# Gate and up products of a two-layer trunk: activation columns streamed from the last to the first, weight buffers placed at four residues of 512 bytes

## The chip, the cores and the metric

The kernel runs on one core of a Trainium2 chip. The metric is the device time of one execution in microseconds (us). Engines are named as in the profile: PE is TensorE's matmul, PEld its weight load, DVE is VectorE, ACT is ScalarE, POOL is GpSimd, SP is the engine that issues most DMAs. A difference of about 2% (20.8 us here) is taken as what tells a change of this kernel from none.

## The reference

Two layers over 256 tokens of width 1024, each layer a SwiGLU block, a mixing block (windowed attention and low-rank attention, gated and merged), and a second SwiGLU block:

```python
def swiglu(x, w_gate, w_up, w_down):
    return (jax.nn.silu(x @ w_gate) * (x @ w_up)) @ w_down

for l in range(DEPTH):                      # DEPTH = 2, D_MODEL = 1024, SEQ = 256, D_FF = 2816
    x = x + 0.5 * swiglu(rms_norm(x, ffn1_norm[l]), ffn1_w_gate[l], ffn1_w_up[l], ffn1_w_down[l])
    h = rms_norm(x, mix_norm[l])
    proj = h @ w_in[l]
    ...
    x = x + merged @ w_out[l]
    x = x + 0.5 * swiglu(rms_norm(x, ffn2_norm[l]), ffn2_w_gate[l], ffn2_w_up[l], ffn2_w_down[l])
```

All values are float32. The gate and up products (`x @ w_gate`, `x @ w_up`), four times in the program, are what the change touches.

## The kernel before

Precision is kept by splitting each float32 operand into a high part, rounded to the type float32r that PE takes in one pass, and a low part, the rest. A product is then three: high by high, low by high and high by low.

A SwiGLU block of D_FF = 2816 is worked in FB = 22 blocks of 128 inner columns. For each block the queue of SP loads 2048 columns of gate and up weights (8 tiles of 128 x 128 for gate, then 8 for up) into `w_raw`, ACT copies them to `w_hi` (function `split_gu`, line 549), and DVE writes the difference to `w_lo` (line 884). Both have two such buffers, slot 0 for even blocks and slot 1 for odd ones, and a third that holds the split weights of the down projection. The transposed activations `hT` hold, for each of the 8 chunks k of 128 model columns, 256 high columns and behind them 256 low ones.

On PE the gate and up products take the weights as the stationary operand and the activations as the moving one, with two helpers. `high` multiplies a `w_hi` tile by all 512 columns of `hT[k]` (in the profile: ps<-hT,w_hi, 128x512) and `low` a `w_lo` tile by the 256 high ones (ps<-hT,w_lo, 128x256). A block has 16 of each. Every product loads its own weights, and all of them are written at line 1369. In the steady loop PE does `gate_up` (16 high, 16 low), `gate_up_low_first` (16 low, 16 high), and two `down` of 12 products each, in which the weights move (ps<-w_hi,aTh and the like, 128x512). The mixing block in between has projections that also move the weights, 512, 416 or 384 columns at a time, over stationary pieces of `hT` or of the attention output `oTh`.

The order of work on every engine is written out by hand, with semaphores between engines; the two slots are what lets ACT, DVE and SP work ahead of PE.

Where the tiles lie in a partition matters here. Tiles are allocated one behind another. In bytes modulo 512, `w_raw`, `w_hi`, `hT`, `aTh` and `aTl` all begin at the same residue, since the sizes ahead of them are multiples of 512. In what follows "offset" is the residue of a tile's address against that common one. A 128 x 128 weight tile takes 512 bytes in a partition, so the tiles of one buffer have one offset. `w_hi` has offset 0, and the gate and up tiles of `w_lo` have 480, by

```python
LO_SHIFT = 120
LO_SLOT = GU_COLS + 128
wl_gu = [w_lo[:, i * LO_SLOT + LO_SHIFT:i * LO_SLOT + LO_SHIFT + GU_COLS] for i in range(2)]
```

while the attention output (`oTh`, its high part, and `oTl`, its low part) and `ident` lie at offset 256.

Of the kernel before, what the change touches and what calls it, by code (L numbers as in the profile page):

```python
# [7 lines left out]
F32 = mybir.dt.float32  # L8
# [89 lines left out]
def build(nc, x_first_in, x_second_in, pos_in, cols_in, rows_in, w_ffn, w_proj, w_gate, w_uq, w_ukv, w_branch, w_out,  # L98
          masks_in, freq_in, out):
    with ExitStack() as ctx:  # L100
# [3 lines left out]
        def signal(name, per_layer, first=0):  # L104
# [8 lines left out]
        raw_gu, wh_gu = ([w[:, i * GU_COLS:(i + 1) * GU_COLS] for i in range(2)] for w in (w_raw, w_hi))  # L113
        wl_gu = [w_lo[:, i * LO_SLOT + LO_SHIFT:i * LO_SLOT + LO_SHIFT + GU_COLS] for i in range(2)]
        raw_d, wh_d = ([w[:, 2 * GU_COLS + i * DN_COLS:2 * GU_COLS + (i + 1) * DN_COLS] for i in range(2)]
                       for w in (w_raw, w_hi))
        wl_d = [w_lo[:, 2 * LO_SLOT + i * DN_COLS:2 * LO_SLOT + (i + 1) * DN_COLS] for i in range(2)]
        mix_raw, mix_hi = ([w[:, i * GU_COLS:(i + 1) * GU_COLS] for i in range(MIX_SLOTS)] for w in (w_raw, w_hi))
        mix_lo = [w_lo[:, i * LO_SLOT:i * LO_SLOT + GU_COLS] for i in range(MIX_SLOTS)]
        hT = sb("hT", [P, KC, 2, SEQ], F32R)  # L120
# [399 lines left out]
        def _(act):  # L520
# [4 lines left out]
            for l in range(DEPTH):  # L525
# [25 lines left out]
                def start_high(i):  # L551

                    act.wait_ge(start_in[i].sem, 16)
                    act.activation(wh_gu[0][:, start_cols(i)], raw_gu[0][:, start_cols(i)], ACT.Copy)\  # L554
                       .then_inc(start_hi.sem if i < 3 else hi_gu.sem, 1)

                def third_high(half):

                    part = slice(half * KC * P, (half + 1) * KC * P)
                    act.wait_ge(third_in.sem, 16)  # L560
                    act.wait_ge(gu_used.sem, gu_used.at(0, 0))
                    act.activation(wh_gu[0][:, part], third_raw[:, part], ACT.Copy)\
                       .then_inc((third_hi, hi_gu)[half].sem, 1)
# [141 lines left out]
                if l == 0:  # L705
# [7 lines left out]
                    for s, (landed, sig) in enumerate(((start_in[4], start_hi), (raw_gu_in[1], hi_gu))):  # L713
                        part = slice(s * KC * P, (s + 1) * KC * P)
                        act.wait_ge(landed.sem, 16)
                        act.activation(wh_gu[1][:, part], raw_gu[1][:, part], ACT.Copy).then_inc(sig.sem, 1)
                    act.wait_ge(ss_clear.sem, 1)
# [151 lines left out]
        def _(dve):  # L869
# [3 lines left out]
            for l in range(DEPTH):  # L873
# [7 lines left out]
                def split_gu(n, i2, e):  # L881
                    b = e % 2
                    dve.wait_ge(hi_gu.sem, i2 + hi_gu.at(n // 2, (0, FFN2_0)[n % 2] + e))
                    dve.tensor_tensor(wl_gu[b], raw_gu[b], wh_gu[b].bitcast(F32), ALU.subtract).then_inc(lo_gu.sem, 1)  # L884

                def split_second(n):

                    for half, sig in enumerate((lo_first, lo_gu)):
                        if n == 0 and half == 0:
                            dve.wait_ge(start_hi.sem, 4)  # L890
                        else:
                            dve.wait_ge(hi_gu.sem, hi_gu.at(n // 2, (0, FFN2_0)[n % 2] + 1))
                        part = slice(half * KC * P, (half + 1) * KC * P)
                        dve.tensor_tensor(wl_gu[1][:, part], raw_gu[1][:, part], wh_gu[1][:, part].bitcast(F32), ALU.subtract)\
                           .then_inc(sig.sem, 1)
# [5 lines left out]
                def third_low(half):  # L901

                    if half == 0:
                        dve.wait_ge(third_hi.sem, 1)
                    else:
                        dve.wait_ge(hi_gu.sem, hi_gu.at(0, 2))
                    part = slice(half * KC * P, (half + 1) * KC * P)
                    ins = dve.tensor_tensor(wl_gu[0][:, part], third_raw[:, part], wh_gu[0][:, part].bitcast(F32), ALU.subtract)
                    ins.then_inc((third_lo, lo_gu)[half].sem, 1)

                def start_low(i):
# [3 lines left out]
                    else:  # L915
                        dve.wait_ge(hi_gu.sem, hi_gu.at(0, 0))
                    dve.tensor_tensor(wl_gu[0][:, start_cols(i)], raw_gu[0][:, start_cols(i)],
                                      wh_gu[0][:, start_cols(i)].bitcast(F32), ALU.subtract)\
                       .then_inc(start_lo.sem if i < 3 else lo_gu.sem, 1)
# [447 lines left out]
        def _(pe):  # L1367
# [17 lines left out]
            for l in range(DEPTH):  # L1385
# [36 lines left out]
                def high(bank, hi, k, first, last=False):  # L1422

                    return mm(ps[:, bank, :], hi, hT[:, k, :, :].rearrange("p s n -> p (s n)"), first, last)

                def low(bank, lo, k, last, first=False):

                    return mm(ps[:, bank, 0:SEQ], lo, hTh[:, k, :], first, last)

                def gate_up(w, i2, e):  # L1430
# [3 lines left out]
                    for s in range(2):  # L1434
                        for k in range(KC):
                            c = (s * KC + k) * P
                            high(2 * b + s, wh_gu[b][:, c:c + P], k, k == 0)
                    pe.wait_ge(lo_gu.sem, i2 + lo_gu.at(l, (0, FFN2_0)[w] + e))
                    for s, sig in enumerate((gate_ps, gu_used)):
                        for k in range(KC):  # L1440
                            c = (s * KC + k) * P
                            ins = low(2 * b + s, wl_gu[b][:, c:c + P], k, k == KC - 1)
                        ins.then_inc(sig.sem, 1)

                def gate_up_low_first(w, i2, e):
# [4 lines left out]
                    for s in range(2):  # L1450
                        for k in range(KC):
                            c = (s * KC + k) * P
                            low(2 * b + s, wl_gu[b][:, c:c + P], k, False, k == 0)
                    for s, sig in enumerate((gate_ps, gu_used)):
                        for k in range(KC):
                            c = (s * KC + k) * P
                            ins = high(2 * b + s, wh_gu[b][:, c:c + P], k, False, k == KC - 1)
                        ins.then_inc(sig.sem, 1)

                def gate_up_last(w, e):  # L1460
# [3 lines left out]
                    for s, sig in enumerate((gate_ps, gu_used)):  # L1464
                        for k in range(KC):
                            c = (s * KC + k) * P
                            high(2 * b + s, wh_gu[b][:, c:c + P], k, k == 0)
                        for k in range(KC):
                            c = (s * KC + k) * P
                            ins = low(2 * b + s, wl_gu[b][:, c:c + P], k, k == KC - 1)  # L1470
                        ins.then_inc(sig.sem, 1)

                def gate_up_first(w):
# [4 lines left out]
                    for k in range(KC):  # L1478
                        if k == 2:
                            columns(l, 2 * w, 1)  # L1480
                        if k == 0:
                            pe.wait_ge(ht_hi.sem, ht_hi.at(l, 2 * w * KC))
                            for s in range(2):
                                c = s * KC * P
                                low(s, wl_gu[0][:, c:c + P], 0, False, True)
                        pe.wait_ge(ht_lo.sem, ht_lo.at(l, 2 * w * KC + k))
                        for s in range(2):
                            c = (s * KC + k) * P
                            high(s, wh_gu[0][:, c:c + P], k, False)
                        if k == 0:  # L1490
                            continue
                        for s, sig in enumerate((gate_ps, gu_used)):
                            c = (s * KC + k) * P
                            ins = low(s, wl_gu[0][:, c:c + P], k, k == KC - 1)
                            if k == KC - 1:
# [3 lines left out]
                def start_high_four(s, half):  # L1499
# [5 lines left out]
                    for k in range(4 * half, 4 * half + 4):  # L1505
                        if s == 0:
                            pe.wait_ge(ht_lo.sem, ht_lo.at(0, k))
                        c = (s * KC + k) * P
                        high(s, wh_gu[0][:, c:c + P], k, k == 0)

                def start_low_four(s, half):
# [5 lines left out]
                    for k in range(4 * half, 4 * half + 4):  # L1517
                        c = (s * KC + k) * P
                        ins = low(s, wl_gu[0][:, c:c + P], k, k == KC - 1)
                    if half == 1:  # L1520
# [20 lines left out]
                def gate_up_second(w):  # L1541

                    for s, sig in enumerate((gate_ps, gu_used)):
# [6 lines left out]
                        for k in range(KC):  # L1550
                            c = (s * KC + k) * P
                            high(2 + s, wh_gu[1][:, c:c + P], k, k == 0)
                            if l + w == 0 and s == 1 and k == 4:
# [3 lines left out]
                        for k in range(KC):  # L1557
                            c = (s * KC + k) * P
                            ins = low(2 + s, wl_gu[1][:, c:c + P], k, k == KC - 1)
                        ins.then_inc(sig.sem, 1)  # L1560
                def gate_up_third():

                    pe.wait_ge(up_sum.sem, up_sum.at(0, 0))
                    for s, sig, hi, lo in ((0, gate_ps, (third_hi.sem, 1), (third_lo.sem, 1)),
                                           (1, gu_used, (hi_gu.sem, hi_gu.at(0, 2)), (lo_gu.sem, lo_gu.at(0, 2)))):
                        pe.wait_ge(*hi)
                        for k in range(KC):
                            c = (s * KC + k) * P
                            high(s, wh_gu[0][:, c:c + P], k, k == 0)
                        pe.wait_ge(*lo)  # L1570
                        for k in range(KC):
                            c = (s * KC + k) * P
                            ins = low(s, wl_gu[0][:, c:c + P], k, k == KC - 1)
                        ins.then_inc(sig.sem, 1)
# [410 lines left out]
```

## Time and profile before

| | us |
|---|---|
| median of 2 runs | 1039.09 (1038.88 to 1039.29) |
| the profiled execution's own time | 1040.34 |
| its span, first to last instruction | 1038.5 |
| PE busy | 1032.4 (99%), 5648 products |
| PE weight loads busy | 891.7 (86%) |
| DVE busy | 718.3 (69%) |
| ACT busy | 586.1 (56%) |

The busy time of PE covers the span, but a product's duration in the profile overlaps that of the next one: what a product costs is the step from its start to the start of the next, and this is what is read below. Times are given to 10 ns in the rows by time, so steps are taken over several products.

### The profile page before, as it was taken

What the parts mean: (1) busy time and instruction counts of PE and PEld (TensorE: products, weight loads), DVE (VectorE), ACT (ScalarE), POOL (GpSimd) and SP (SyncE); (2) the same over time, 40 slices, a digit from 0 to 9 for tenths busy, and PEclk for the clock granted to TensorE, in tenths of its full rate; (3) what the DMA queues carried; (4) which work ended last, traced back from release to release, by engine and by line L of the source; (5) the groups of instructions that cost most, each with busy time, mean ns of one, the idle gap of its engine ahead of it and who ended that gap; (6) DMA issues with size and microseconds to landing.
All of it is one profiled execution on the core that took longest, in us unless ns stands there. A gap on an engine that the chain in (4) does not pass through costs nothing.

```text
span 1038.5 us, 15559 instructions
## 1 busy us (share of the span) xinstructions
PE 1032.4 (99%) x5648; PEld 891.7 (86%) x5648; DVE 718.3 (69%) x1132; ACT 586.1 (56%) x935; POOL 61.8 (6%) x71
## 2 busy tenths in 40 slices
PE   8999999999999999999999999999999999999998
PEld 7888888998888888888888888889988888888887
DVE  6766666668786876666687666666688868666665
ACT  6555454466963754554565455455678646454552
POOL 0052000121100000000000000001211000000000
PEclk9999999999999999999999999999999999999999
DMA  7665544455435455655445555534454346545541
GB/s 264 248 225 192 204 162 167 140 183 193 146 123 203 173 187 189 205 189 209 179 147 202 202 192 182 210 136 152 154 203 163 122 163 219 205 163 202 191 173 61
DMA packets 35269, 187.53 MB, mean 181 GB/s; under 512 B 4368, under 2 KB 4384, under 8 KB 20128
## 3 DMA queue, kind: packets, MB, share of 16 engines
q1 hardware_dynamic: 34992, 186.51, 51.0%
q0 software_dynamic: 240, 0.53, 0.2%
q8 instruction: 23, 0.38, 0.1%
q14 instruction: 14, 0.11, 0.0%
HBM read 185.98 MB, written 1.05 MB: 180 GB/s over the span
## 4 chain that ended last, share of the span: by engine, by line
PE 99%; DMA 1%; SPq 0%; DVE 0%; ACT 0%; issue 0%
PE ps L1369 96%; PE ps L1803 1%; PE ps L1393 1%; DMA w_raw<-in_w_ffn 1%; PE ps L1832 1%; PE ps L1868 0%; PE ps L1712 0%; PE ps L1704 0%; PE ps L1414 0%; DVE x_cols L999 0%; ACT w_hi L554 0%; SPq L318 0%; SPq L317 0%
## 5 line engine op out<-in xcount | busy, mean ns | idle before, releaser
L1369 PE MATMUL ps<-hT,w_hi 128*128 128x512 f32 x1408 | 341.3, 391 | 1.9 <-ACT w_hi L554 1.9
L1369 PEld LDWEIGHTS ps<-hT,w_hi 128*128 128x128 f32 x1408 | 258.9, 188 | 52.4 <-ACT w_hi L554 2.1
L884 DVE TENSOR_TENSOR w_lo<-w_raw,w_hi 128x2048 fp32r<-128x2048 f32 x82 | 188.0, 2293 | 87.7 <-ACT w_hi L549 87.7
L1369 PEld LDWEIGHTS ps<-hT,w_lo 128*128 128x128 f32 x1408 | 176.8, 188 | 7.5
L1369 PE MATMUL ps<-hT,w_lo 128*128 128x256 f32 x1408 | 178.3, 279 | 0.0
L1369 PE MATMUL ps<-w_hi,hT 128*128 128x512 f32 (+2 forms) x576 | 174.3, 377 | 0.0
L549 ACT ACTIVATE w_hi<-w_raw 128x2048 fp32r<-128x2048 f32 x85 | 162.0, 1906 | 13.9 <-PE ps L1369 13.2
L1369 PE MATMUL ps<-w_lo,aTh 128*128 128x512 f32 x352 | 137.2, 390 | 0.0
L1369 PE MATMUL ps<-w_hi,aTl 128*128 128x512 f32 x352 | 137.0, 389 | 0.0
L1369 PE MATMUL ps<-w_hi,aTh 128*128 128x512 f32 x352 | 136.8, 390 | 0.0
L578 ACT ACTIVATE S<-ps 128x256 f32<-128x256 f32 x88 | 33.7, 383 | 154.6 <-PE ps L1369 154.6
L1369 PEld LDWEIGHTS ps<-w_hi,hT 128*128 128x128 f32 x576 | 107.2, 188 | 15.9 <-DVE w_lo L878 1.3
L878 DVE TENSOR_TENSOR w_lo<-w_raw,w_hi 128x2048 fp32r<-128x2048 f32 (+3 forms) x50 | 94.9, 1905 | 33.6 <-ACT w_hi L537 33.3
L537 ACT ACTIVATE w_hi<-w_raw 128x2048 fp32r<-128x2048 f32 (+3 forms) x54 | 86.0, 1592 | 52.0 <-PE ps L1369 49.8
L572 ACT ACTIVATE w_hi<-w_raw 128x1024 fp32r<-128x1024 f32 x88 | 92.9, 1055 | 38.4 <-PE ps L1369 38.4
L1369 PE MATMUL ps<-w_lo,hT 128*128 128x512 f32 (+2 forms) x288 | 107.5, 373 | 0.0
L940 DVE TENSOR_TENSOR w_lo<-w_raw,w_hi 128x1024 fp32r<-128x1024 f32 x88 | 104.4, 1219 | 1.4 <-ACT w_hi L572 1.4
L946 DVE TENSOR_TENSOR S<-ps,S 128x256 f32<-128x256 f32 x88 | 37.1, 421 | 84.9 <-ACT S L578 84.8
L1369 PEld LDWEIGHTS ps<-w_hi,aTl 128*128 128x128 f32 x352 | 66.1, 188 | 13.9
L1369 PEld LDWEIGHTS ps<-w_hi,aTh 128*128 128x128 f32 x352 | 66.1, 188 | 13.5
L1369 PEld LDWEIGHTS ps<-w_lo,aTh 128*128 128x128 f32 x352 | 66.1, 188 | 13.0
L584 ACT ACTIVATE work<-work 128x256 f32<-128x256 f32 x88 | 36.7, 417 | 68.5 <-DVE work L953 68.5
(168 smaller groups left out, 952.9 us busy)
## 6 DMA issues: line engine op xcount, KB each, us to landing
w_raw<-in_w_ffn SPq DMA_DIRECT2D x85, 1024.0 KB, 4.9
w_raw<-in_w_ffn SPq DMA_DIRECT2D x90, 512.0 KB, 5.7
w_raw<-in_w_gate SPq DMA_DIRECT2D x16, 1024.0 KB, 5.1
w_raw<-in_w_proj SPq DMA_DIRECT2D x16, 592.0 KB, 4.4
w_raw<-in_w_branch SPq DMA_DIRECT2D x8, 1024.0 KB, 4.8
w_raw<-in_w_out SPq DMA_DIRECT2D x8, 1024.0 KB, 4.8
w_raw<-in_w_uq SPq DMA_DIRECT2D x4, 384.0 KB, 3.0
w_raw<-in_w_ffn SPq DMA_DIRECT2D x4, 256.0 KB, 6.6
```

The costliest lines, as they stand in the source:

```text
L537: act.activation(mix_hi[m][:, 0:ncols], mix_raw[m][:, 0:ncols], ACT.Copy).then_inc(hi_gu.sem, 1)
L549: act.activation(wh_gu[b], raw_gu[b], ACT.Copy).then_inc(hi_gu.sem, 1)
L572: act.activation(wh_d[b], raw_d[b], ACT.Copy).then_inc(hi_d.sem, 1)
L578: act.activation(folded[:, b, 0, :], ps[:, 2 * b, SEQ:2 * SEQ], ACT.Copy).then_inc(g_low.sem, 1)
L584: act.activation(silu[:, b, :], silu[:, b, :], ACT.Silu).then_inc(silu_done.sem, 1)
L878: dve.tensor_tensor(mix_lo[m][:, 0:ncols], mix_raw[m][:, 0:ncols], mix_hi[m][:, 0:ncols].bitcast(F32), ALU.subtract).then_inc(lo_gu.sem, 1)
L884: dve.tensor_tensor(wl_gu[b], raw_gu[b], wh_gu[b].bitcast(F32), ALU.subtract).then_inc(lo_gu.sem, 1)
L940: dve.tensor_tensor(wl_d[b], raw_d[b], wh_d[b].bitcast(F32), ALU.subtract).then_inc(lo_d.sem, 1)
L946: dve.tensor_tensor(folded[:, b, 0, :], ps[:, 2 * b, 0:SEQ], folded[:, b, 0, :], ALU.add)\
L1369: return pe.matmul(dst, w, m, start=start, stop=stop, skip_group_check=True)
L1393: ins = pe.transpose(dst[:, t * P:(t + 1) * P], x[:, c // 4, t, c % 4 * P:(c % 4 + 1) * P], ident[:, :])
L1803: ins = pe.transpose(ps[:, 4 + h % 4, s * P:(s + 1) * P], S[:, h, s * P:(s + 1) * P], ident[:, :])
```

## The change

Three things change in the code, and all of them concern only the gate and up products.

- `high` and `low` read the activations from the last column to the first, and write their outputs in PSUM in the same reversed order, so each result stands where it stood before.
- `w_hi` gets the padded slots that `w_lo` had (2176 columns, 17 times 512 bytes, in place of 2048), and in both buffers the eight gate tiles and the eight up tiles of a slot begin at places of their own: offset 0 for gate and 256 for up in slot 0, offset 128 for gate and 384 for up in slot 1. The offset of 480 in `w_lo` is gone.
- Since gate and up no longer follow each other without a gap, the ACT copy and the DVE difference over 2048 columns write (and read) `w_hi` and `w_lo` in two pieces of 1024. The tiles behind `w_hi` move by 1536 bytes, three times 512, so no other offset changes.

```diff
-LO_SHIFT = 120
-LO_SLOT = GU_COLS + 128
+HI_AT, LO_AT = ((0, 64), (32, 96)), ((0, 64), (32, 96))
+PART_SLOT = GU_COLS + 128
...
-        w_hi = sb("w_hi", [P, MIX_SLOTS * GU_COLS], F32R)
-        w_lo = sb("w_lo", [P, MIX_SLOTS * LO_SLOT], F32R)
...
+        w_hi = sb("w_hi", [P, MIX_SLOTS * PART_SLOT], F32R)
+        w_lo = sb("w_lo", [P, MIX_SLOTS * PART_SLOT], F32R)
+        raw_gu = [w_raw[:, i * GU_COLS:(i + 1) * GU_COLS] for i in range(2)]
+
+        def halves(w, i, gate_at, up_at):
+
+            step = KC * P + up_at - gate_at
+            a = i * PART_SLOT + gate_at
+            return w[:, a:a + 2 * step].rearrange("p (s n) -> p s n", s=2)[:, :, 0:KC * P]
+
+        def cols_of(w, c, n):
+
+            return w[:, c // (KC * P), c % (KC * P):c % (KC * P) + n]
+
+        wh_gu, wl_gu = ([halves(w, i, *at) for i, at in enumerate(places)] for w, places in ((w_hi, HI_AT), (w_lo, LO_AT)))
...
-                    act.activation(wh_gu[b], raw_gu[b], ACT.Copy).then_inc(hi_gu.sem, 1)
+                    act.activation(wh_gu[b], raw_gu[b].rearrange("p (s n) -> p s n", s=2), ACT.Copy).then_inc(hi_gu.sem, 1)
...
-                    dve.tensor_tensor(wl_gu[b], raw_gu[b], wh_gu[b].bitcast(F32), ALU.subtract).then_inc(lo_gu.sem, 1)
+                    dve.tensor_tensor(wl_gu[b], raw_gu[b].rearrange("p (s n) -> p s n", s=2), wh_gu[b].bitcast(F32), ALU.subtract).then_inc(lo_gu.sem, 1)
...
-                    return mm(ps[:, bank, :], hi, hT[:, k, :, :].rearrange("p s n -> p (s n)"), first, last)
+                    return mm(ps[:, bank, :][:, ::-1], hi, hT[:, k, :, :].rearrange("p s n -> p (s n)")[:, ::-1], first, last)
...
-                    return mm(ps[:, bank, 0:SEQ], lo, hTh[:, k, :], first, last)
+                    return mm(ps[:, bank, 0:SEQ][:, ::-1], lo, hTh[:, k, :][:, ::-1], first, last)
```

All other edits put `cols_of` where a slice of `wh_gu` or `wl_gu` stood. No instruction is added, removed or moved on any engine: the lists of PE, POOL and SP are the same, and those of ACT and DVE differ only in the shape of the splits of 2048 columns. In ACT's list, in the loop of a SwiGLU block (`aTh` is the high part of the down projection's activations, S and work are scratch tiles), there stands before

```order
46 L549 ACTIVATE w_hi<-w_raw 128x2048
47 L597 ACTIVATE aTh<-work 128x256
48 L577 REGISTER_ALU
49 L578 ACTIVATE S<-ps 128x256
50 L589 REGISTER_ALU
51 L590 ACTIVATE S<-ps 128x256
```

and now

```order
46 L560 ACTIVATE w_hi<-w_raw 128x2x1024
47 L608 ACTIVATE aTh<-work 128x256
48 L588 REGISTER_ALU
49 L589 ACTIVATE S<-ps 128x256
50 L600 REGISTER_ALU
51 L601 ACTIVATE S<-ps 128x256
```

The instruction keeps its place and its neighbours, and only its form and the line numbers differ.

## Rows read from the trace of the kernel before

**Rows 1.** The page's head: busy time of each engine, and the granted clock by slices.

```profile
span 1038.5 us, 15559 instructions
PE 1032.4 (99%) x5648; PEld 891.7 (86%) x5648; DVE 718.3 (69%) x1132; ACT 586.1 (56%) x935; POOL 61.8 (6%) x71
...
PEclk9999999999999999999999999999999999999999
```

**Rows 2.** The page's chain of work that ended last, by engine and line.

```profile
PE 99%; DMA 1%; SPq 0%; DVE 0%; ACT 0%; issue 0%
PE ps L1369 96%; PE ps L1803 1%; PE ps L1393 1%; DMA w_raw<-in_w_ffn 1%; PE ps L1832 1%; PE ps L1868 0%; PE ps L1712 0%; PE ps L1704 0%; PE ps L1414 0%; DVE x_cols L999 0%; ACT w_hi L554 0%; SPq L318 0%; SPq L317 0%
```

**Rows 3.** All waits of PE: waiter, releaser, us in total, times, longest.

```profile
PE ps L1369 <- ACT w_hi L554: 1.9, 1, 1.9
PE ps L1380 <- DVE kTA L870: 1.0, 1, 1.0
```

**Rows 4.** The page's groups of the gate and up products and of their splits.

```profile
L1369 PE MATMUL ps<-hT,w_hi 128*128 128x512 f32 x1408 | 341.3, 391 | 1.9 <-ACT w_hi L554 1.9
...
L884 DVE TENSOR_TENSOR w_lo<-w_raw,w_hi 128x2048 fp32r<-128x2048 f32 x82 | 188.0, 2293 | 87.7 <-ACT w_hi L549 87.7
...
L1369 PE MATMUL ps<-hT,w_lo 128*128 128x256 f32 x1408 | 178.3, 279 | 0.0
...
L549 ACT ACTIVATE w_hi<-w_raw 128x2048 fp32r<-128x2048 f32 x85 | 162.0, 1906 | 13.9 <-PE ps L1369 13.2
```

**Rows 5.** PE by time, one turn of the loop: start us, us, products.

```profile
154.71 3.80 PE L1369 MATMUL ps<-hT,w_hi 128*128 128x512 f32 x16
158.34 3.90 PE L1369 MATMUL ps<-hT,w_lo 128*128 128x256 f32 x32
162.08 3.81 PE L1369 MATMUL ps<-hT,w_hi 128*128 128x512 f32 x16
165.73 0.39 PE L1369 MATMUL ps<-w_hi,aTh 128*128 128x512 f32 x1
...
171.17 3.80 PE L1369 MATMUL ps<-hT,w_hi 128*128 128x512 f32 x16
```

**Rows 6.** PE by time: mixing block, 384 columns a product.

```profile
202.41 0.51 PE L1369 MATMUL ps<-w_hi,hT 128*128 128x384 f32 x2
...
205.53 0.51 PE L1369 MATMUL ps<-w_hi,hT 128*128 128x384 f32 x2
```

**Rows 7.** PE by time: weights over `oTh` and `oTl`, which lie at offset 256.

```profile
303.14 0.39 PE L1369 MATMUL ps<-w_hi,oTl 128*128 128x512 f32 x1
...
305.86 0.39 PE L1369 MATMUL ps<-w_hi,oTl 128*128 128x512 f32 x1
```

**Rows 8.** Transposes of 128 columns on PE: two runs of twelve by time.

```profile
275.03 1.48 PE L1803 MATMUL ps<-ident,S 128*128 128x128 f32 x12
...
296.36 1.47 PE L1803 MATMUL ps<-ident,S 128*128 128x128 f32 x12
```

**Rows 9.** PE by line and form: all those transposes, busy us, mean ns.

```profile
L1803 PE MATMUL ps<-ident,S 128*128 128x128 f32 x96 | 11.8, 272 | 0.0
```

**Rows 10.** Writers of `oTh` (one piece of 512) and `hT` (two of 256): ns min/median/max.

```profile
L810 ACT ACTIVATE oTh<-ps x8: 574/594/598, 283.2 to 814.6; 128x512 fp32r<-128x512 f32 x8
L1275 DVE TENSOR_TENSOR oTl<-ps,oTh x8: 684/688/692, 285.7 to 815.3; 128x512 fp32r<-128x512 f32 x8
...
L853 ACT ACTIVATE hT<-ps x8: 594/596/598, 312.2 to 835.7; 128x512 fp32r<-128x512 f32 x8
L1305 DVE TENSOR_TENSOR hT<-ps,hT x8: 680/686/692, 312.8 to 836.5; 128x512 fp32r<-128x512 f32 x8
```

**Rows 11.** Busy time by stretch, that loop turn: PE, PEld, DVE, ACT, POOL, clock, DMA.

```profile
154.71:171.17 16.46, 16.46 (x90) 14.25 (x88) 10.75 (x15) 8.49 (x12) 0.00 (x0) 1.00 0.56 193
```

**Rows 12.** ACT and DVE by time: the split of the block that PE begins at 171.17.

```profile
161.40 1.91 ACT L549 ACTIVATE w_hi<-w_raw 128x2048 fp32r<-128x2048 f32 x1
...
163.34 2.29 DVE L884 TENSOR_TENSOR w_lo<-w_raw,w_hi 128x2048 fp32r<-128x2048 f32 x1 [0.85 <-ACT w_hi L549]
```

More of the change, by code:

```diff
@@ L110, in build @@
         w_raw = sb("w_raw", [P, MIX_SLOTS * GU_COLS])
-        w_hi = sb("w_hi", [P, MIX_SLOTS * GU_COLS], F32R)
-        w_lo = sb("w_lo", [P, MIX_SLOTS * LO_SLOT], F32R)
[L113 to L119, printed above, removed]
+        w_hi = sb("w_hi", [P, MIX_SLOTS * PART_SLOT], F32R)
[8 more added lines that the diff above has]
+        wh_gu, wl_gu = ([halves(w, i, *at) for i, at in enumerate(places)] for w, places in ((w_hi, HI_AT), (w_lo, LO_AT)))
+        raw_d = [w_raw[:, 2 * GU_COLS + i * DN_COLS:2 * GU_COLS + (i + 1) * DN_COLS] for i in range(2)]
+        wh_d, wl_d = ([w[:, 2 * PART_SLOT + i * DN_COLS:2 * PART_SLOT + (i + 1) * DN_COLS] for i in range(2)]
+                      for w in (w_hi, w_lo))
+        mix_raw = [w_raw[:, i * GU_COLS:(i + 1) * GU_COLS] for i in range(MIX_SLOTS)]
+        mix_hi, mix_lo = ([w[:, i * PART_SLOT:i * PART_SLOT + GU_COLS] for i in range(MIX_SLOTS)] for w in (w_hi, w_lo))
         hT = sb("hT", [P, KC, 2, SEQ], F32R)
@@ L561, in third_high @@
                     act.wait_ge(gu_used.sem, gu_used.at(0, 0))
-                    act.activation(wh_gu[0][:, part], third_raw[:, part], ACT.Copy)\
+                    act.activation(cols_of(wh_gu[0], part.start, KC * P), third_raw[:, part], ACT.Copy)\
                        .then_inc((third_hi, hi_gu)[half].sem, 1)
@@ L715, in _ @@
                         act.wait_ge(landed.sem, 16)
-                        act.activation(wh_gu[1][:, part], raw_gu[1][:, part], ACT.Copy).then_inc(sig.sem, 1)
+                        act.activation(cols_of(wh_gu[1], part.start, KC * P), raw_gu[1][:, part], ACT.Copy).then_inc(sig.sem, 1)
                     act.wait_ge(ss_clear.sem, 1)
@@ L893, in split_second @@
                         part = slice(half * KC * P, (half + 1) * KC * P)
-                        dve.tensor_tensor(wl_gu[1][:, part], raw_gu[1][:, part], wh_gu[1][:, part].bitcast(F32), ALU.subtract)\
+                        dve.tensor_tensor(cols_of(wl_gu[1], part.start, KC * P), raw_gu[1][:, part], cols_of(wh_gu[1], part.start, KC * P).bitcast(F32), ALU.subtract)\
                            .then_inc(sig.sem, 1)
@@ L907, in third_low @@
                     part = slice(half * KC * P, (half + 1) * KC * P)
-                    ins = dve.tensor_tensor(wl_gu[0][:, part], third_raw[:, part], wh_gu[0][:, part].bitcast(F32), ALU.subtract)
+                    ins = dve.tensor_tensor(cols_of(wl_gu[0], part.start, KC * P), third_raw[:, part], cols_of(wh_gu[0], part.start, KC * P).bitcast(F32), ALU.subtract)
                     ins.then_inc((third_lo, lo_gu)[half].sem, 1)
@@ L1466, in gate_up_last @@
                             c = (s * KC + k) * P
-                            high(2 * b + s, wh_gu[b][:, c:c + P], k, k == 0)
+                            high(2 * b + s, cols_of(wh_gu[b], c, P), k, k == 0)
                         for k in range(KC):
                             c = (s * KC + k) * P
-                            ins = low(2 * b + s, wl_gu[b][:, c:c + P], k, k == KC - 1)
+                            ins = low(2 * b + s, cols_of(wl_gu[b], c, P), k, k == KC - 1)
                         ins.then_inc(sig.sem, 1)
@@ L1488, in gate_up_first @@
                             c = (s * KC + k) * P
-                            high(s, wh_gu[0][:, c:c + P], k, False)
+                            high(s, cols_of(wh_gu[0], c, P), k, False)
                         if k == 0:
```

30 lines of the change are left out of this document (15 added, 15 removed).

## The prediction

> **What bounds the kernel now.** I read the page's head first: PE is busy for 1032.4 of 1038.5 us, DVE for 69%, ACT for 56%, and the granted clock is at its upper level of 2.4 GHz all through [rows 1]. The chain that ended last is PE for 99%, with 96% at the one line that writes the products [rows 2]. PE waits for other engines 2.9 us in the whole program, both times at its start [rows 3]. So the time is the sum of PE's steps from one product to the next, and only what changes such a step can change it. Of its 5648 products 1408 are high and 1408 low ones of gate and up [rows 4].
>
> The time line gives the steps. In the loop 16 high products take 158.34 - 154.71 = 3.63 us, 227 ns each; 32 low ones 3.74 us, 116.9 ns each; 16 high ones behind them 3.65 us, 228 ns; 24 down products 171.17 - 165.73 = 5.44 us, 226.7 ns [rows 5]. At 2.4 GHz 512 columns are 213.3 ns and 256 are 106.7 ns. Each product therefore costs more than its columns: 13.5 ns for 512 and 10.2 ns for 256. This excess is all that the change can touch, since it leaves the columns and the number of products alone. So gate and up take 1408 x 227.3 + 1408 x 116.9 = 320 + 165 = 485 us, of which 19 + 14 = 33 us are excess.
>
> What makes the excess? During a product PE loads the weights of the next one, so two streams read SBUF at once: the moving columns, and 128 weight columns. That they cross in a bank or port is one reading. Four rows bear on it. First, 384 moving columns take (205.53 - 202.41) / 18 = 173.3 ns, also 13.3 ns over their 160.0 [rows 6]: the excess belongs to the product and not to its length. Second, with moving weights at offset 0 and the next stationary piece at offset 256 the step is (305.86 - 303.14) / 12 = 226.7 ns [rows 7], the same as in the down products where both are at offset 0: half of 512 bytes makes no difference when columns are read upward. Third, the low products are the only ones at offset 480, and the only ones with an excess of 10.2 in place of 13.4. Fourth, transposes of plain float32 have 128 columns and step by (1.47 - 0.27) / 11 = 109.1 ns in one run and 110.0 in another, where 0.27 is the duration of the last one [rows 8, 9]. If that step is the load of 128 columns, at half the moving columns' rate (106.7 ns), its excess is 2.4 ns: this one type of product has almost none.
>
> **The change part by part.**
>
> 1. The offset 480 goes. The low products now have offsets 0, 256, 128 and 384. For 0 and 256 the rows say an excess of 13.3 to 13.5 ns at two other lengths, 384 and 512; for 128 and 384 there is no row. Bounds: 0 if the 3.3 ns that the low products save come from their length alone and not from the offset, and 1408 x (13.5 - 10.2) = +4.6 us if they come from the offset. I take the upper one, since every product that has an offset of 0 or 256 and the float32r type, whatever its length, shows the full 13.4. Effect: +4.6 us.
>
> 2. The high products go from offset 0 to the four. Read upward, 0 and 256 are equal to 0.3 ns, so 0 for half of them, and I take 0 for 128 and 384 as well, the middle between those. Bounds are those of part 3.
>
> 3. The direction. No product of the trace reads or writes downward, so the price is bounded from both sides. Below: the excess goes down to the 2.4 ns of the transposes. That is (227.3 - 215.7) x 1408 = -16.3 us for high and (116.9 - 109.1) x 1408 = -11.0 us for low, -27.3 us in all. Above: if a downward column cost two clock steps in place of one, 213.3 and 106.7 ns more for each product, 1408 x 320 = +450 us. Between these ends I take 0. The excess is a fixed cost of the load, equal at 384 and 512 columns and at two offsets, and the load reads the same 128 columns at the same rate either way.
>
> A rule of the Trainium skill would decide parts 1 to 3 at once. The page SBUF — State Buffer, section Who interferes with whom, gives PE two read ports, one for the moving operand and one for the weight load, independent of each other. By that rule neither offset nor direction could matter, and the time would stay at 1039.1; but the time line shows an excess that differs between the two kinds of product [rows 5], which that rule alone does not explain.
>
> 4. The splits in two pieces. The nearest rows are pairs with the same number of columns: ACT writes 512 to `oTh` in one piece in 594 ns and to `hT` in two pieces in 596; DVE takes 688 and 686 [rows 10]. So a second piece costs 2 ns at most, 85 x 2 + 82 x 2 = 0.3 us on engines that are idle for 8.0 and 5.7 us of a turn of 16.46 [rows 11]. The cover is large: the split of slot 0 ends at 163.31 on ACT and 165.63 on DVE, and PE reads it from 171.17 on [rows 12], 7.9 and more than 5.5 us later. Nothing on the path. If that cover were gone, a split would cost its 1.9 + 2.3 us for each of 88 blocks, but the shortest cover shrinks only by what PE gains: 27 us over the 44 pairs of blocks are 0.6 us a turn, and DMA is busy for 0.56 of it [rows 11].
>
> 5. `w_hi` is larger by 1536 bytes a partition and the tiles behind it move by three times 512. No offset of the down products or of the mixing block changes: 0.
>
> Sum against the profiled execution: 1040.3 + 4.6 + 0 + 0 = 1044.9 us, 0.4% more. That execution stands 1.25 us above the median of the runs, 1039.1 us, on which the same sum gives **1043.7 us**.
>
> **The rivals.**
>
> *The streams stop getting in each other's way.* Read downward, the activations run in the same direction as the weight load, if that load goes from its last column to its first, and the different placements keep them apart. The excess then falls, at most by the 27.3 us of part 3, to 1011.8; at half the effect, 1039.1 - 13.7 = 1025.4. For it: the low products show that offset can change the excess (rows 5). Against: no row has a smaller excess than 10 ns for float32r, at three lengths and three offsets. More than 2% faster needs 76% of the excess above 2.4 ns gone.
>
> *The streams run side by side and lock.* This is the case on the other side. The load takes 106.7 ns for 128 columns, half the rate of the moving columns. In opposite directions they pass quickly. In the same one, where they start in the same bank, the moving stream could be held behind the load until it is done: it would make 128 of 256 columns in that time, 53.3 ns lost in place of 13.5, +39.8 ns a product. If one of the four placements does this, 704 of 2816 products, that is +28.0 us, with +3.5 us for the low products of the rest: 1070.6 us. It decides (20.8 us) from 523 locked products on. For it: the sole offset that differs now already changes the excess, so position counts. Against: at offset 0 or 256 there is no sign of it upward.
>
> *A column read or written downward is slow.* +450 us, 1489 us, from the estimate of two clock steps a column above. The Trainium skill, page Advanced Engine Details and Errata, section Memory Cachelines, says that any access in PSUM that isn't contiguous slows matmuls down markedly. Whether a step of -1 counts as contiguous there, no run here shows yet. Against it: every product of the kernel before steps by +1, so nothing for it either.
>
> *Nothing of it acts*, offset or direction (the change doesn't do what it says): 1039.1 us, the low products staying at 116.9.
>
> **How the numbers follow.** Forecast 0.45; streams kept apart 0.27, of it 0.16 beyond 2%; locked 0.13, of it 0.10 beyond 2%; slow columns 0.07; nothing acts 0.08. Predicted is the likeliest, 1043.7 us. The range holds the two sides of the unknown direction, from the full gain, 1012, to one locked placement, 1070; left out are the slow columns and the locks of more than one placement, some 0.12. Faster by over 2%: 0.16. Slower: 0.10 + 0.07 = 0.17. Within: 0.67. As 2% is about what tells a change from none, most of what I expect isn't told apart by it.
>
> **What would show it.** In the profile after, the loop's blocks of 16 high products should take 3.63 us still, and 32 low ones 3.84 (120.2 ns each) in place of 3.74. If all gate and up steps are near 216 and 109 ns, the first rival is right; if blocks of one slot or of gate alone are longer (267 ns a product), the second; 440 ns a product, the third; 116.9 for low, the last. Down products stay at 226.7, the splits at 1906 and 2293 ns. The prediction is wrong if the direction acts on the excess at all, which I set at 0 without a row.

## The result, and the profile after

The changed kernel takes 1052.0 us (1051.84 to 1052.20) against 1039.1: a ratio of 1.0121, with a 95% interval of 1.0105 to 1.0138. It is 12.9 us slower: inside the stated range, and nearly three times the growth that was forecast (4.6 us), and the interval excludes the forecast of 1.0044.

PE still bounds the kernel. The page's head and its group rows of the changed kernel, whose line numbers are 11 higher:

```profile
span 1050.0 us, 15559 instructions
PE 1044.4 (99%) x5648; PEld 895.7 (85%) x5648; DVE 718.2 (68%) x1132; ACT 586.0 (56%) x935; POOL 61.8 (6%) x71
...
L1380 PE MATMUL ps<-hT,w_hi 128*128 128x512 f32 x1408 | 349.2, 398 | 1.3 <-ACT w_hi L565 1.3
...
L895 DVE TENSOR_TENSOR w_lo<-w_raw,w_hi 128x2048 fp32r<-128x2048 f32 x82 | 188.0, 2293 | 87.1 <-ACT w_hi L560 87.1
...
L1380 PE MATMUL ps<-hT,w_lo 128*128 128x256 f32 x1408 | 181.7, 282 | 0.0
...
L560 ACT ACTIVATE w_hi<-w_raw 128x2048 fp32r<-128x2048 f32 x85 | 161.8, 1904 | 13.4 <-PE ps L1380 13.2
```

Against [rows 1] and [rows 4] DVE, ACT and POOL are busy for the same time to 0.1 us, the splits in two pieces last 2293 and 1904 ns where they lasted 2293 and 1906, and the span grew by 11.5 us. (Against its own median the profiled execution of before was 1.25 us high; that is why spans differ by 11.5 and medians by 12.9.) All waits of PE in the changed kernel:

```profile
PE ps L1380 <- ACT w_hi L565: 1.3, 1, 1.3
PE ps L1391 <- DVE kTA L881: 1.1, 1, 1.1
```

So no wait took the time: 2.4 us, as short as in [rows 3]. It lies in the steps. PE by time in one turn of the loop of the changed kernel, to be set beside [rows 5]:

```profile
139.88 3.90 PE L1380 MATMUL ps<-hT,w_hi 128*128 128x512 f32 x16
143.62 3.98 PE L1380 MATMUL ps<-hT,w_lo 128*128 128x256 f32 x32
147.43 3.90 PE L1380 MATMUL ps<-hT,w_hi 128*128 128x512 f32 x16
151.16 0.40 PE L1380 MATMUL ps<-w_hi,aTh 128*128 128x512 f32 x1
...
156.62 3.90 PE L1380 MATMUL ps<-hT,w_hi 128*128 128x512 f32 x16
```

From start to start: 16 high products in 3.74 us (3.63 before), 32 low ones in 3.81 (3.74), 16 high ones in 3.73 (3.65), 24 down products in 5.46 (5.44). The gate and up products of a pair of blocks take 0.26 us more, and 44 pairs give 11.4 us, the whole growth of the span. By kind, from the starts of all products in the two traces: 1408 high ones 322.1 to 329.8 us (+7.7), 1408 low ones 164.2 to 167.7 (+3.5). Once a block has settled, each high product steps by 233.3 to 233.5 ns at each of the four offsets, against 226.7 before. (The first few of a block differ: before, in the blocks whose low products come first, the steps begin at 233, 236, 229, 232 and 231 ns and then stay at 227.)

### The profile page after: what moved, and what is told of

Same layout as the page of the kernel before. It is cut to its first block, busy times and chain, and to the rows that moved or that the text cites. A ratio compares the mean times of both kernels' runs of the same rounds, so it can differ in the third digit from the quotient of the medians.

```text
span 1050.0 us, 15559 instructions
## 1 busy us (share of the span) xinstructions
PE 1044.4 (99%) x5648; PEld 895.7 (85%) x5648; DVE 718.2 (68%) x1132; ACT 586.0 (56%) x935; POOL 61.8 (6%) x71
## 4 chain that ended last, share of the span: by engine, by line
PE 99%; DMA 1%; SPq 0%; DVE 0%; ACT 0%; issue 0%
PE ps L1380 96%; PE ps L1814 1%; PE ps L1404 1%; DMA w_raw<-in_w_ffn 1%; PE ps L1843 0%; PE ps L1879 0%; PE ps L1723 0%; PE ps L1715 0%; PE ps L1425 0%; DVE x_cols L1010 0%; ACT w_hi L565 0%; SPq L329 0%; SPq L328 0%
## 5 line engine op out<-in xcount | busy, mean ns | idle before, releaser
L1380 PE MATMUL ps<-hT,w_hi 128*128 128x512 f32 x1408 | 349.2, 398 | 1.3 <-ACT w_hi L565 1.3
L895 DVE TENSOR_TENSOR w_lo<-w_raw,w_hi 128x2048 fp32r<-128x2048 f32 x82 | 188.0, 2293 | 87.1 <-ACT w_hi L560 87.1
L1380 PEld LDWEIGHTS ps<-hT,w_lo 128*128 128x128 f32 x1408 | 179.5, 188 | 7.9
L1380 PE MATMUL ps<-hT,w_lo 128*128 128x256 f32 x1408 | 181.7, 282 | 0.0
L560 ACT ACTIVATE w_hi<-w_raw 128x2048 fp32r<-128x2048 f32 x85 | 161.8, 1904 | 13.4 <-PE ps L1380 13.2
L1380 PEld LDWEIGHTS ps<-w_lo,aTh 128*128 128x128 f32 x352 | 66.1, 188 | 13.3
```

Source lines behind the costliest of these rows:

```text
L560: act.activation(wh_gu[b], raw_gu[b].rearrange("p (s n) -> p s n", s=2), ACT.Copy).then_inc(hi_gu.sem, 1)
L895: dve.tensor_tensor(wl_gu[b], raw_gu[b].rearrange("p (s n) -> p s n", s=2), wh_gu[b].bitcast(F32), ALU.subtract).then_inc(lo_gu.sem, 1)
L1380: return pe.matmul(dst, w, m, start=start, stop=stop, skip_group_check=True)
```

## The experiments

Every run kept the order of instructions on PE, and the granted clock was 1.00 in each. "Up" is from the first column to the last, "down" the other way. "High" and "low" below are mean steps over all products of a kind, or over those at one offset, from their starts in the trace; before they are 228.7 and 116.6 ns over all, and a settled high product takes 226.7. The kernel before was timed again beside each group, at 1039.3 to 1039.5 us.

| run | reads, writes | offsets high / low | us | ratio, 95% interval |
|---|---|---|---|---|
| after | down, down | 0, 256, 128, 384 both | 1052.0 | 1.0105 to 1.0138 |
| offsets_only | up, up | 0, 256, 128, 384 both | 1045.2 | 1.0036 to 1.0069 |
| reversed_only | down, down | 0 / 480 | 1050.1 | 1.0080 to 1.0114 |
| read_down | down, up | 0 / 480 | 1049.3 | 1.0076 to 1.0110 |
| write_down | up, down | 0 / 480 | 1039.2 | 0.9989 to 1.0008 |
| low_at_0 | up, up | 0 / 0 | 1042.9 | 1.0022 to 1.0047 |
| high_at_480 | up, up | 480 / 480 | 1048.1 | 1.0068 to 1.0102 |
| fours_down | fours down, up | 0 / 480 | 1049.6 | 1.0078 to 1.0118 |
| inside_fours_down | down in fours, up | 0 / 480 | 1039.4 | 0.9991 to 1.0011 |
| sixteens_down | sixteens down, up | 0 / 480 | 1052.2 | 1.0095 to 1.0153 |
| sixty_fours_down | 64s down, up | 0 / 480 | 1039.5 | 0.9990 to 1.0012 |
| scan_a | up, up | 32, 64, 96, 160 both | 1050.3 | 1.0077 to 1.0135 |
| scan_b | up, up | 448, 480, 16, 496 both | 1044.6 | 1.0030 to 1.0076 |
| all_shifted | up, up | 0 / 480, `hT` moved too | 1042.2 | 1.0016 to 1.0038 |
| down_weights_down | down products down | 0 / 480 | 1047.1 | 1.0058 to 1.0089 |
| low_at_64 | up, up | 0 / 64 | 1040.2 | 0.9999 to 1.0017 |

### One part at a time: offsets, direction, reading, writing

offsets_only is the changed kernel with `high` and `low` as before:

```diff
-                    return mm(ps[:, bank, :][:, ::-1], hi, hT[:, k, :, :].rearrange("p s n -> p (s n)")[:, ::-1], first, last)
+                    return mm(ps[:, bank, :], hi, hT[:, k, :, :].rearrange("p s n -> p (s n)"), first, last)
...
-                    return mm(ps[:, bank, 0:SEQ][:, ::-1], lo, hTh[:, k, :][:, ::-1], first, last)
+                    return mm(ps[:, bank, 0:SEQ], lo, hTh[:, k, :], first, last)
```

> The changed kernel with the activations read and the outputs written upward again; the four offsets stay. In the changed kernel the steady step of a high product is 233.4 ns at each of the offsets 0, 256, 128 and 384, against 226.7 before, and the low ones take 118 to 120 ns against 116.7. If the direction is what costs (theory A), high goes back to 226.7 at all four offsets and low stays above 116.9, at about 120, by the loss of the offset 480: 1039.1 + 4.6 = 1043.7 us or less. If the offsets cost (theory B), the time stays near 1052. If the offset 480 did nothing either (theory C), it is 1039 again.

reversed_only is the other half: the kernel before with this diff the other way round.

> The kernel before with the reading and writing downward alone; w_hi at offset 0 and w_lo at 480 as before. Theory A (direction costs, per product and whatever the offset): high 233.4 ns, 1408 x 6.7 = +9.4 us less the disturbed products, so about +8 us, 1047, plus or minus what low does. Theory B (offsets cost): 1039. If direction and offset only cost together: 1039 here and in the run with the offsets alone.

read_down and write_down take half of that each; the diff of read_down for `high`:

```diff
-                    return mm(ps[:, bank, :], hi, hT[:, k, :, :].rearrange("p s n -> p (s n)"), first, last)
+                    return mm(ps[:, bank, :], hi, hT[:, k, :, :].rearrange("p s n -> p (s n)")[:, ::-1], first, last)
```

> The kernel before with the activations read downward and the outputs written upward, so that the tokens of the gate and up results stand in reverse order: a timing experiment only. If it is the read from SBUF that costs (theory A1, it runs alongside the weight load), about 1047 us with high at 233.4 ns. If it is the write to PSUM (theory A2), 1039 with high at 226.7.

and of write_down:

```diff
-                    return mm(ps[:, bank, :], hi, hT[:, k, :, :].rearrange("p s n -> p (s n)"), first, last)
+                    return mm(ps[:, bank, :][:, ::-1], hi, hT[:, k, :, :].rearrange("p s n -> p (s n)"), first, last)
```

> The kernel before with the activations read upward and the outputs written downward; the tokens of the gate and up results stand in reverse order, a timing experiment only. Theory A1 (the read costs): 1039 us, high at 226.7 ns. Theory A2 (the write costs): about 1047 us, high at 233.4 ns. If each costs half, 1043 in both runs.

The direction costs 10.7 us alone, the offsets 5.7, both together 12.9: once the read is reversed, the offsets add only 2.2. The whole cost of the direction is in the read: 1049.3 us with the read alone and 1039.2 with the write alone, in which high and low keep their 228.7 and 116.6 ns. PE by time in read_down, then in write_down:

```profile
156.46 3.90 PE L1369 MATMUL ps<-hT,w_hi 128*128 128x512 f32 x16
160.20 3.93 PE L1369 MATMUL ps<-hT,w_lo 128*128 128x256 f32 x32
163.97 3.90 PE L1369 MATMUL ps<-hT,w_hi 128*128 128x512 f32 x16
```

```profile
154.28 3.80 PE L1369 MATMUL ps<-hT,w_hi 128*128 128x512 f32 x16
157.91 3.90 PE L1369 MATMUL ps<-hT,w_lo 128*128 128x256 f32 x32
161.65 3.82 PE L1369 MATMUL ps<-hT,w_hi 128*128 128x512 f32 x16
```

The first pair of steps is 3.74 and 3.77 us, the second 3.63 and 3.74, as in [rows 5]. With both reversed, in reversed_only, it is that of the read alone:

```profile
140.00 3.90 PE L1369 MATMUL ps<-hT,w_hi 128*128 128x512 f32 x16
143.73 3.93 PE L1369 MATMUL ps<-hT,w_lo 128*128 128x256 f32 x32
147.50 3.90 PE L1369 MATMUL ps<-hT,w_hi 128*128 128x512 f32 x16
```

16 high products take 3.73 us (233 ns), 32 low ones 3.77 (117.8 ns). And in offsets_only:

```profile
154.80 3.79 PE L1380 MATMUL ps<-hT,w_hi 128*128 128x512 f32 x16
158.43 3.97 PE L1380 MATMUL ps<-hT,w_lo 128*128 128x256 f32 x32
162.24 3.88 PE L1380 MATMUL ps<-hT,w_hi 128*128 128x512 f32 x16
165.96 0.39 PE L1380 MATMUL ps<-w_hi,aTh 128*128 128x512 f32 x1
```

Here slot 0, at offsets 0 and 256, keeps its 3.63 us for 16 high products, slot 1, at 128 and 384, takes 3.72, and the 32 low products take 3.81. By offset (a half is the eight gate or the eight up products of one kind in a block), high within a half takes 227.2 ns at 0 and 226.9 at 256, but 233.0 at 128 and 232.8 at 384. That explains why the parts don't add up: read downward, a high product takes 233.3 to 233.5 ns at any of the four offsets, 6.7 more than upward at 0 and 256 but at most 1.5 more than upward at 128 and 384. Those two cost 5 to 6 ns upward, and downward there is nothing left for them to take. For low products the offset takes most: 164.2 us before, 167.6 with the offsets alone, 165.9 with the direction alone, 167.7 with both.

### The two kinds of weights at other offsets

low_at_0 changes one constant; high_at_480 is offsets_only with another table:

```diff
-LO_SHIFT = 120
+LO_SHIFT = 0
...
-HI_AT, LO_AT = ((0, 64), (32, 96)), ((0, 64), (32, 96))
+HI_AT, LO_AT = ((120, 120), (120, 120)), ((120, 120), (120, 120))
```

> The kernel before with LO_SHIFT = 0: the low weights at offset 0 in place of 480, everything upward. The run with the four offsets took 5.7 us more than before, 3.4 of it in the low products. If the offset 480 is what saves there (theory A), every low product at offset 0 steps by 120.0 ns against 116.6 and the time is 1039.4 + 1408 x 3.3 ns = 1044 us. If the cost in that run came only from the offsets 128 and 384 (theory B), or from offsets that change between gate and up (theory C), it is 1039.4.

> The kernel before with the high weights at offset 480 as well as the low ones, everything upward. Theory A (480 is a good offset for both kinds): high falls by 3 ns to about 223, 1039.4 - 4 = 1035 us. Theory B (a high product settles on 226.7 wherever the load does not lie at an odd multiple of 128): 1039.4, high at 226.7. Theory C (every offset but 0 and 256 costs a high product, as 128 and 384 did): high at 233, 1039.4 + 8 = 1047 us.

PE by time in low_at_0:

```profile
154.65 3.79 PE L1369 MATMUL ps<-hT,w_hi 128*128 128x512 f32 x16
158.28 4.00 PE L1369 MATMUL ps<-hT,w_lo 128*128 128x256 f32 x32
162.11 3.82 PE L1369 MATMUL ps<-hT,w_hi 128*128 128x512 f32 x16
```

32 low products take 3.83 us, 119.7 ns each, where 480 gave 3.74: the padding of 480 bytes was worth 3.6 us, and the forecast's +4.6 for its loss is confirmed in kind (low products 164.2 to 168.3 us, +4.1, and 0.5 less in the high ones). For the high products, 480 is as bad as 128: 233.7 ns, 1048.1 us, theory C. PE by time in high_at_480:

```profile
155.18 3.89 PE L1380 MATMUL ps<-hT,w_hi 128*128 128x512 f32 x16
158.91 3.90 PE L1380 MATMUL ps<-hT,w_lo 128*128 128x256 f32 x32
```

16 high products take 3.73 us, and the 32 low ones, from 158.91 to 162.65, keep their 3.74. What helps one kind hurts the other.

### Which order of the read costs

Four kernels read the activations in blocks of b columns, by

```diff
-hTh[:, k, :]
+hTh[:, k, :].rearrange("p (a b) -> p a b", b=4)[:, ::-1, :]
```

and likewise for the 512 columns of `high`; inside_fours_down has `[:, :, ::-1]` in that place, sixteens_down and sixty_fours_down have b=16 and b=64.

> The kernel before with the activations read in groups of four columns (16 bytes), the groups from the last to the first, upward inside each; outputs written upward, so the tokens of gate and up stand in another order: a timing experiment only. Reading all columns downward cost 9.9 us, high 233.4 ns. Theory A (what costs is the order of the 16-byte groups, against the weight load that reads at the same time): 1049 us again. Theory B (what costs is the order inside a group): 1039.4. Any break in the run of addresses may cost on its own: then well above 1049, by 128 breaks a product.

> The kernel before with the activations read in groups of four columns, the groups from the first to the last, downward inside each; outputs written upward, a timing experiment only. Theory A (the order of the groups costs): 1039.4 us, high at 226.7 ns. Theory B (the order inside a group costs): 1049 us, high at 233.4. If both orders cost half, 1044 in this run and in the one with the groups downward.

> The kernel before with the activations read in blocks of 64 columns (256 bytes), the blocks from the last to the first, upward inside each; outputs upward, so tokens stand in another order: a timing experiment only. Upward reading doesn't tell an offset of 256 from 0, so if the cost comes from where the two reads stand against each other modulo 256 bytes (theory A), this looks like upward reading: 1039.4 us, high 226.7. If any downward order costs (theory B), 1049.5 us, high 233.4, as with groups of four columns.

> As the run before it, in blocks of 16 columns (64 bytes) from the last to the first; a timing experiment only. Theory A (places modulo 256 bytes count): the order within 256 bytes is now another, so a cost, about 1049 us, unless the pattern is coarser than 64 bytes. Theory A2 (places modulo 64 bytes count): 1039.4. Theory B (any downward order): 1049.5 us.

fours_down equals read_down product by product (high 234.1 and low 117.8 in both), and inside_fours_down equals the kernel before. So reversing inside 16 bytes is free, and reversing the 16-byte groups costs everything. With 64-byte blocks (sixteens_down) the high products pay in full again, 234.0 ns, and the low ones pay more than in any other run, 119.8 against 117.8 in fours_down; the run takes 1052.2 us, 2.6 more than that one. PE by time in sixteens_down:

```profile
156.28 3.90 PE L1369 MATMUL ps<-hT,w_hi 128*128 128x512 f32 x16
160.01 4.00 PE L1369 MATMUL ps<-hT,w_lo 128*128 128x256 f32 x32
163.85 3.90 PE L1369 MATMUL ps<-hT,w_hi 128*128 128x512 f32 x16
```

With 256-byte blocks the cost is gone. PE by time in sixty_fours_down, whose eight blocks run from the last to the first:

```profile
154.11 3.80 PE L1369 MATMUL ps<-hT,w_hi 128*128 128x512 f32 x16
157.75 3.90 PE L1369 MATMUL ps<-hT,w_lo 128*128 128x256 f32 x32
161.48 3.82 PE L1369 MATMUL ps<-hT,w_hi 128*128 128x512 f32 x16
```

3.64 and 3.73 us, as in [rows 5]. Going down in steps of 256 bytes costs nothing, and neither do breaks in the run of addresses, 127 of them in inside_fours_down. What costs lies within 256 bytes, the same period by which 0 and 256 are alike for a high product that reads upward.

Whether it is the order itself isn't shown. Each order that costs also starts elsewhere: counted in bytes modulo 512, the plain downward read and fours_down begin in the 16-byte group at 496 and sixteens_down at 448, while the free ones begin in the group at 0 (inside_fours_down) or at 256 (sixty_fours_down). The weights of the high products are then 16 or 64 bytes off the first column read, and an upward read with weights 16 or 64 bytes off pays as much (the scan below: 233.1 and 233.7 ns). So for the high products "where the read begins against the weights" fits every run here as well as "in which order it goes". A downward read with the weights at 240 or 496 would tell the two apart, and no run has it. The low products of sixteens_down speak against the start alone: they begin 32 bytes off their weights and take 119.8 ns, where an upward read at 32 takes 118.2.

### Scanning the offset

scan_a and scan_b are offsets_only with four other offsets each:

```diff
-HI_AT, LO_AT = ((0, 64), (32, 96)), ((0, 64), (32, 96))
+HI_AT, LO_AT = ((8, 16), (24, 40)), ((8, 16), (24, 40))
...
+HI_AT, LO_AT = ((112, 120), (4, 124)), ((112, 120), (4, 124))
```

> The changed kernel read and written upward, with four other offsets for high and low weights alike: 32 and 64 for gate and up of slot 0, 96 and 160 for slot 1. High products upward took 226.7 ns at 0 and 256, 232 to 233 at 128, 384 and 480. Theory A (the high product is free of the extra 6 ns only near multiples of 256): all four between 227 and 234, none below 226. Theory B (some offset keeps the two reads apart and the excess vanishes): one of them near 216 to 220 ns. Low products: 116.6 at 480 and 120.0 at 0; by theory A all four between 116 and 121. Total by A about 1045 to 1049 us.

> As the run before it, with offsets 448 and 480 for gate and up of slot 0, and 16 and 496 for slot 1. Theory A: at 480 high 233.5 and low 116.8 as measured; 16 and 496 lie nearer to 0, so high between 226.7 and 233, low between 116.8 and 120. Theory B: one of them well below 226. Total by A about 1044 to 1048 us.

Mean steps within a half, upward (good to some 0.5 ns), from these two runs and from offsets_only (0, 256, 128, 384):

| offset | 0 | 16 | 32 | 64 | 96 | 128 | 160 | 256 | 384 | 448 | 480 | 496 |
|---|---|---|---|---|---|---|---|---|---|---|---|---|
| high, ns | 227.2 | 233.1 | 233.0 | 233.7 | 234.9 | 233.0 | 233.4 | 226.9 | 232.8 | 229.4 | 233.4 | 228.5 |
| low, ns | 118.9 | 118.0 | 118.2 | 116.3 | 119.8 | 118.1 | 118.7 | 120.0 | 119.1 | 117.7 | 117.8 | 118.3 |

Theory A held in its lower bound (none below 226), and not in its picture: 96 lies above its upper bound of 234 ns, 16 pays in full though it is next to 0, and scan_a took 1050.3 us where 1049 was the most expected. A high product is at its best at 0 and 256 alone. 16 bytes above 0 the cost is full; 16 bytes below (496) it is 1.6 ns and 64 below (448) 2.5. No offset removes the excess. A half has only 8 products, and its neighbours lie at other offsets: 480 reads 117.8 for low here and 116.6 to 116.9 where all low products have it. That a half carries over how the one before it ended is the likely reason, and no run isolates it.

### What remained open: relative place, and other products

low_at_64 is offsets_only with a table; all_shifted has another table and pads around `hT`; down_weights_down reverses the moving weights and the outputs of the down products:

```diff
+HI_AT, LO_AT = ((0, 0), (0, 0)), ((16, 16), (16, 16))                 # low_at_64
...
+HI_AT, LO_AT = ((32, 32), (32, 32)), ((24, 24), (24, 24))             # all_shifted
+        pad_a = sb("pad_a", [P, 32])
         hT = sb("hT", [P, KC, 2, SEQ], F32R)
+        pad_b = sb("pad_b", [P, 96])
...
+            def down_by_weight(dst, ah, al, wh, wl, start, stop):         # down_weights_down
+                dst, wh, wl = dst[:, ::-1], wh[:, ::-1], wl[:, ::-1]
+                return act_by_weight(dst, ah, al, wh, wl, start, stop)
```

> The kernel before, all upward, with the activations hT moved by 128 bytes and the high and low gate and up weights moved by 128 as well, so that their offsets against hT stay at 0 and 480 while each address is another modulo 512. Theory A (the place of the weight load against the moving columns counts): high 226.7 ns and low 116.8, 1039.3 us, plus what the mixing block pays, whose 864 products read moving weights against stationary pieces of hT, now 128 apart: at most 864 x 6 ns = 5 us. Theory B (the residue of the address itself counts, or the split into padded slots): high at 233 ns, 1047 us or more.

> The kernel before with the moving weights of the 1056 down products read from the last column to the first and their outputs written likewise; gate and up as before. Theory A (any float32r product pays 6.7 ns when its moving operand runs in the direction in which the load reads): down products at 233.4 ns, 1056 x 6.7 = +7.1 us, 1046.4. Theory B (it comes from the activations' layout in hT): 1039.3.

> The kernel before, upward, with the low weights at offset 64 in place of 480 and the high ones at 0. Low products at 64 stepped by 116.3 ns in the scan, against 116.8 at 480. If that holds for all of them, -0.7 us: 1038.6, hardly to be told from 1039.3; if what surrounds them decides, the same within 1 us.

all_shifted moved both streams of gate and up by 128 bytes, and PE by time shows the steps of before:

```profile
154.40 3.80 PE L1382 MATMUL ps<-hT,w_hi 128*128 128x512 f32 x16
158.04 3.90 PE L1382 MATMUL ps<-hT,w_lo 128*128 128x256 f32 x32
161.77 3.82 PE L1382 MATMUL ps<-hT,w_hi 128*128 128x512 f32 x16
```

All high products take 322.5 us (322.1 before) and all low ones 164.3 (164.2). Moving the weights alone by 128 had cost the high ones 6 ns each. So it is the place of the weight tile against the moving columns that counts, and for this shift not the address. The 2.9 us that the run lost are mostly in the mixing block, where `hT` is the stationary side and now lies 128 bytes off: 864 products, +2.4 us.

down_weights_down lost 7.8 us: products that had nothing to do with the change, at 228.0, 227.4 and 226.8 ns, went to 234.0, 234.1 and 233.1, +6.7 of the 7.1 us expected. low_at_64 is no better than the kernel before (1.0008, 0.9999 to 1.0017); the 116.3 of one half in scan_a became 117.7 over all. No kernel beat the one before.

## Why the prediction was wrong

**The failed step is part 3, the direction, taken as 0.** Measured: reading downward added 9.9 us (read_down), 7.5 of it in the high products (5.3 ns each over all, 6.7 once they have settled) and 1.7 in the low ones (1.2 each); writing downward added nothing. The reason given was that the excess is a fixed cost of the load, "equal at 384 and 512 columns and at two offsets". The two offsets were 0 and 256, the only two of twelve that are alike and good, so the evidence for "offset makes no difference" was two samples of one case. What the rows did show and I passed over is that the excess of the low products differed at a third offset: the excess then depends on how two address streams stand to each other, and turning one of them round changes just that. The trace of before had one more such sign: the products of 416 columns in the mixing block step by 188.0 ns, 14.7 over their 173.3, so the excess wasn't the same at every length either.

**Part 1, the offset 480,** was right: +4.6 forecast, +3.6 measured by itself, in the low products, which settle at 120.0 ns at offset 0 upward, 13.3 over their 106.7 as the rows for 384 and 512 columns said. In the change itself, where the read is reversed, losing 480 costs the low products less: 165.9 us in reversed_only, 167.7 in the changed kernel.

**Part 2, the high products at four offsets,** was wrong with the same cause: 0 was right for 0 and 256, and 128 and 384 cost 5 to 6 ns a product. It shows only upward (high +2.3 us in offsets_only), since downward all offsets cost alike.

**Parts 4 and 5** held. Splits in two pieces cost nothing measurable, and nothing else moved. The bounds of part 3, -27.3 and +450 us, held the 9.9; the value chosen between them did not. That the total of 1052.0 lies in the range says little for the sum: the range was that wide because no row priced the direction.

**The rivals.** Streams that come apart: no offset, direction or block order brought high below 226 ns. The lock was right in that the reversed read loses, and wrong in shape: 6.7 ns at all four placements alike, not 39.8 at one of them. Its picture needs a load that runs downward, which no run shows. Slow downward columns: excluded, for the write too. By the rule of the Trainium skill (SBUF — State Buffer, Who interferes with whom) of two independent read ports, neither offset nor direction could matter. The measurement differs: low_at_64 and high_at_480 are one program but for the offsets of the weights, and a settled high product took 226.7 ns in the one and 233 in the other. Whether the two reads meet at those ports or elsewhere, no run shows. The rule of the Trainium skill on PSUM (Advanced Engine Details and Errata, Memory Cachelines), that access which isn't contiguous slows matmuls down, doesn't reach a step of -1: write_down took 1039.2 us.

What stays open is the mechanism below the byte pattern: why a high product loses 13.3 ns at the best placement and 20 at others, and whether the downward read pays for its order or for where it begins. Two tests are missing: a downward read with the weights shifted to match its start, and a weight load turned round. A load that runs downward, crossed by the upward read and accompanied by the downward one, is a picture that was only argued.

## What to carry to other kernels

Where PE is the bound and each product loads new weights, look at where the stationary tile lies against the moving one. Here 16 bytes made 6 ns, and places 256 bytes apart were alike where both were tried (0 and 256, 128 and 384). For 512 moving columns keep the two at the same residue of 256; for other lengths measure, since 256 columns were at their best elsewhere. Read the moving operand upward unless a run shows that your order is free: here no reversed read was faster than the upward one. When a view shows that a small cost differs with placement, don't price another change of placement at zero from two samples that agree.

## What the runs showed of the hardware

- A float32r product of 512 moving columns with its own weight load stepped by 226.7 ns (settled) at offsets 0 and 256, and by 228.5 to 234.9 at ten others, against 213.3 for its columns at 2.4 GHz.
- Moving activations and weights together by 128 bytes left the steps as they were (high 322.5 against 322.1 us over all, low 164.3 against 164.2); moving the weights alone cost high products 5 to 6 ns.
- Reading the moving operand downward, or in 16-byte groups or 64-byte blocks from the last to the first, cost a settled product of 512 columns 6 to 7 ns against upward at offset 0, in gate and up as in the down products (downward only there); reversing within 16 bytes, or the order of 256-byte blocks, cost nothing. Against upward at 128 or 384 the downward read cost at most 1.5 ns.
- Writing 512 or 256 columns of PSUM from the last to the first cost nothing (write_down: ratio 0.9998, 0.9989 to 1.0008).
- For products of 256 columns the best placement of the three tried for all of them was another: 480 (116.6 ns), against 64 (117.7) and 0 (119.5).
